# A hybrid attention, recurrence and gated feed-forward block: w_mod's sums moved out of the first and last pair, the out product finished row tile by row tile, and the rows of up begun among the transposes

## The reference

```python
mod = silu(c) @ w_mod + b_mod                      # 2048 x 12288
sh1, sc1, g1, sh2, sc2, g2 = split(mod, 6)         # 2048 numbers each
h = rms_norm(x, pre_mix_norm) * (1 + sc1) + sh1
q_a, k_a, v_a, f_b, q_b, i_b, g_b, gate_a, gate_b = split(h @ w_in)
y_a = sliding_window_sink_attention(q_a, k_a, v_a) @ w_branch_a
y_b = hgrn2_output(hgrn2_chunkwise(q_b, f_b, i_b), g_b) @ w_branch_b
merged = sigmoid(gate_a) * y_a + sigmoid(gate_b) * y_b
x = x + g1 * rms_norm(merged @ w_out, post_mix_norm)
h = rms_norm(x, pre_ffn_norm) * (1 + sc2) + sh2
a, b = split(h @ w_up)                             # 5504 columns each
y = (gelu(conv3(a) + conv_b) * b) @ w_down
x = x + g2 * rms_norm(y, post_ffn_norm)
```

## Time and profile before

| | |
|---|---|
| median of 3 runs | 2906.93 us (2905.8 to 2908.78) |
| the profiled execution | 2907.6 us, span 2905.9 us |
| mean granted TensorE clock | 0.986 |
| TensorE busy | 2820.5 us (97%), 13213 matmuls |
| VectorE busy | 1478.0 us (51%) |
| ScalarE busy | 1012.6 us (35%) |
| GpSimd busy | 36.6 us (1%) |
| HBM | 130 GB/s over the span |

### The profile page before, as it was taken

How to read it: one execution, slowest core, us unless ns; L and a number is a source line. 1 busy time by engine, 2 the same in 40 slices (tenths; PEclk the granted TensorE clock), 3 DMA queues, 4 the chain that set the end, 5 groups by cost and what they waited for, 6 DMA issues and landing times.

```text
span 2905.9 us, 36602 instructions
## 1 busy us (share of the span) xinstructions
PE 2820.5 (97%) x13213; PEld 2355.6 (81%) x13213; DVE 1478.0 (51%) x2011; ACT 1012.6 (35%) x1315; POOL 36.6 (1%) x74
## 2 busy tenths in 40 slices
PE   5999999999899999999989999999999999999997
PEld 5788888888788888878778888888888887888886
DVE  7857777778866666652253333333333333333334
ACT  4344444444422222232253333333333332323323
POOL 0030000000000000000000000000000000000000
PEclk8999999999899999999989999999999999999999
DMA  9842222223577777763233333333333334223222
GB/s 363 290 124 80 77 77 79 80 80 88 152 211 218 215 216 216 221 228 101 87 135 97 94 100 95 94 101 94 94 100 94 96 99 150 96 94 101 94 94 100
DMA packets 451695, 379.56 MB, mean 131 GB/s; under 512 B 20252, under 2 KB 376867, under 8 KB 448817
## 3 DMA queue, kind: packets, MB, share of 16 engines
q1 hardware_dynamic: 438624, 357.61, 40.2%
q0 software_dynamic: 3104, 16.93, 1.6%
q10 hardware_dynamic: 9904, 4.26, 0.6%
HBM read 368.25 MB, written 10.50 MB: 130 GB/s over the span
## 4 chain that ended last, share of the span: by engine, by line
PE 94%; DVE 3%; issue 1%; ACT 1%; DMA 1%; SPq 0%; DVEq 0%; ACTq 0%
PE acc_bank L480 24%; PE acc_bank L482 24%; PE acc_bank L481 24%; PE two_banks L480 2%; PE two_banks L481 2%; PE two_banks L482 2%; PE bank_pb L480 1%; PE bank_pb L481 1%; PE bank_tb L480 1%; PE bank_pb L482 1%; PE bank_ta L480 1%; PE bank_tb L481 1%; PE bank_tb L482 1%; PE bank_ta L481 1%; PE bank_ta L482 1%
## 5 line engine op out<-in xcount | busy, mean ns | idle before, releaser
L456 DVE TENSOR_TENSOR w_lo<-raw,w_hi 128x1024 fp32r<-128x1024 f32 x466 | 570.0, 1223 | 1235.7 <-ACT w_hi L450 1235.6
L450 ACT CAST w_hi<-raw 128x1024 fp32r<-128x1024 f32 x466 | 490.0, 1052 | 1491.7 <-PE acc_bank L482 972.7
L480 PE MATMUL acc_bank<-h_hi,w_hi 128*128 128x512 f32 x2500 | 983.5, 393 | 6.4 <-DVE h_lo L1287 6.4
L482 PE MATMUL acc_bank<-h_hi,w_lo 128*128 128x512 f32 x2500 | 975.0, 390 | 0.0
L481 PE MATMUL acc_bank<-h_lo,w_hi 128*128 128x512 f32 x2500 | 974.4, 390 | 0.0
L480 PEld LDWEIGHTS acc_bank<-h_hi,w_hi 128*128 128x128 f32 x2500 | 470.7, 188 | 101.3 <-issue 6.5
L482 PEld LDWEIGHTS acc_bank<-h_hi,w_lo 128*128 128x128 f32 x2500 | 470.1, 188 | 98.8
L481 PEld LDWEIGHTS acc_bank<-h_lo,w_hi 128*128 128x128 f32 x2500 | 470.7, 188 | 95.5
L1273 DVE SCALAR_TENSOR_TENSOR acc<-raw,csil,acc 128x512 f32<-128x512 f32 x240 | 180.0, 750 | 14.2 <-DMA raw<-in_w_mod_dram 7.6
L480 PE MATMUL acc_bank<-w_hi,a_hi 128*128 128x512 f32 x258 | 100.5, 389 | 2.8 <-DVE w_lo L456 2.8
L480 PE MATMUL acc_bank<-o_hi,w_hi 128*128 128x512 f32 x256 | 102.2, 399 | 0.8 <-DVE w_lo L456 0.8
(11 more groups left out here) (374 smaller groups left out, 3176.7 us busy)
## 6 DMA issues: line engine op xcount, KB each, us to landing
raw<-in_w_ffn_up_dram SPq DMA_DIRECT2D x172, 512.0 KB, 3.7
raw<-in_w_in_dram SPq DMA_DIRECT2D x148, 512.0 KB, 4.0
raw<-in_w_mod_dram SPq DMA_DIRECT2D x128, 512.0 KB, 4.5
raw<-in_w_ffn_down_dram SPq DMA_DIRECT2D x86, 512.0 KB, 3.6
mods_low<-in_w_mod_dram SPq DMA_DIRECT2D x32, 512.0 KB, 9.6
raw<-in_w_out_dram SPq DMA_DIRECT2D x32, 512.0 KB, 3.8
mods_hi<-in_w_mod_dram SPq DMA_DIRECT2D x16, 512.0 KB, 9.8
mods_lo<-in_w_mod_dram SPq DMA_DIRECT2D x16, 512.0 KB, 9.8
```

The lines of the kernel that those rows point to most:

```text
L450: act.copy(w_pair(g)[0][:], raw[n % RAW][:]).then_inc(hi_ready, 1)
L456: dve.tensor_tensor(w_l[:], raw[n % RAW][:], w_h[:].bitcast(F32), ALU.subtract).then_inc(lo_ready, 1)
L480: pe.matmul(o, stat[0], mov[0], start=start, stop=False)
L482: return pe.matmul(o, stat[1], mov[0], start=False, stop=stop)
```

## The change

* **w_mod.** Pair 0 and pair 7 carry no w_mod; pair 7 leaves the loop. Pairs 1 to 6 carry the 96 pieces of g1, sh2 and sc2.
* **g2 in up.** The 32 pieces of g2 are loaded by POOL, one in each of up's passes 1 to 32, into `small[:, 2:4]` (`g2_in`), issued when VectorE's products of the pass before are done. VectorE clears `gain2` and adds the products of four groups into its four quarters (`g2_piece`, between `w_lo` of pieces 0 and 1). After up, TensorE sums all 16 columns; at the start of down, VectorE forms `gcol`, TensorE transposes it at the fifth bank, ScalarE copies it to `acc` ahead of its split of the second piece, and POOL stores it and reads it back.
* **Out's last group.** Its first three pieces run as before. The last five have weight pairs of their own (three lie where h was) and are gone through once for each row tile, so that tile 0's sums are complete after 30 of 120 matmuls. Squares, products, root, inverse, x2, its squares and its root run tile by tile.
* **Transposed rows.** VectorE multiplies x2 itself by the inverse root (in place, once its store has landed; tile 3 in quarters into `x2_last`), and TensorE makes plain transposes into six banks. `diag` is gone.
* **Up's first pass.** Pieces 0 and 1 of up have weight pairs of their own and are split while tile 3 is normed. The rows of a and b are multiplied k by k, with the transposes of block kb + 6 behind those of kb.

```diff
 N2 = N1 + HEADS * HEAD_PIECES
-N3 = N2 + KT // 2 * (PAIR_PIECES + PAIR_MODS)
+MODS_PAIRS = 6
+NM = N2 + PAIR_PIECES - (PAIR_PIECES + PAIR_MODS)
+N3 = N2 + KT // 2 * PAIR_PIECES + MODS_PAIRS * PAIR_MODS
+MODS_LAST = MODS_HEAD + MODS_PAIRS * PAIR_MODS
+SUMS_LAST = MODS_LAST // 8
...
+            if OUT_KEPT < g < P4 - 1:
+                return RH[1]["out_hi"][:, g - OUT_KEPT - 1], RH[1]["out_lo"][:, g - OUT_KEPT - 1]
+            if g == P4 - 1:
+                return w_hi[OUT_KEPT % SPL - 1], w_lo[OUT_KEPT % SPL - 1]
+            if P4 <= g < P4 + 2:
+                return RO[5]["up_hi"][:, g - P4], RO[5]["up_lo"][:, g - P4]
             return w_hi[g % SPL], w_lo[g % SPL]
...
+        def pair_free(g, looped=0):
+
+            if not looped:
+                if OUT_KEPT < g < P4 - 1:
+                    return P3
+                if g == P4 - 1:
+                    return OUT_KEPT
+                if P4 <= g < P4 + 4:
+                    return P4
...
+            pair(0, True, False)
+            with pe.Fori(1, KT // 2 - 1) as it:
                 pair(it, False)
...
+            pair(KT // 2 - 1, False, False)
+
+            def turn_gains(n):
+
+                pe.wait_ge(gcol_ready, n + 1)
+                pe.transpose(SC1[0:KT, 0:P], gcol[:, n, :], ident[:]).then_inc(gcol_turned, 1)
...
+            out_group(P3, even_free(0), 0)
+            out_group(P3 + 8, odd_free, 1)
+            out_group(P3 + 16, even_free(1), 0)
+            out_group(P3 + 24, last_free, 1, 3)
+
+            for t4 in range(TT):
+                for g in range(OUT_KEPT, P4):
+                    if t4 == 0:
+                        pe.wait_ge(lo_ready, g + 1)
+                    wh, wl = weights(g, 2)
+                    for k in range(2):
+                        kb = 2 * (g - P3 - 24) + k
+                        mm = three(OUT_BANKS[1][t4], (m_hi[:, kb, t4 * P:(t4 + 1) * P], m_lo[:, kb, t4 * P:(t4 + 1) * P]),
+                                   (wh[:, k, :], wl[:, k, :]), False, kb == KT - 1)
+                    if t4 == TT - 1:
+                        mm.then_inc(multiplied, 1)
+                if t4 < TT - 1:
+                    mm.then_inc(y1_done, 1)
+
...
+            def turn(kb, i):
+                if i == TT - 1 and kb % 4 == 0:
+                    pe.wait_ge(x2n_ready, TT + kb // 4)
+                src = x2_last if i == TT - 1 else y1[:, i, :]
+                return pe.transpose(TURN6[kb % 6][:, i * P:(i + 1) * P], src[:, kb * P:(kb + 1) * P], ident[:])
+
...
+            pe.wait_ge(y1_out, 16)
+            for i in range(TT - 1):
+                pe.wait_ge(x2n_ready, i + 1)
+                for kb in range(5):
+                    turn(kb, i)
             pe.wait_ge(y1_out, 17)
...
+            for i in range(TT - 1):
+                turn(5, i)
+            for kb in range(6):
+                turn(kb, TT - 1).then_inc(h2_turned, 1)
+
+            def up_rows(b, kb):
+                g = P4 + 2 * (kb // 8) + b
+                wh, wl = weights(g, 8)
+                mm = three(A[b][:], (wh[:, kb % 8, :], wl[:, kb % 8, :]), (h_hi[:, kb, :], h_lo[:, kb, :]), kb == 0, kb == KT - 1)
+                if kb % 8 == 7:
+                    mm.then_inc(multiplied, 1)
+
+            pe.wait_ge(lo_ready, P4 + 2)
+            for kb in range(8):
+                pe.wait_ge(h2_ready, kb + 1)
+                up_rows(0, kb)
+                up_rows(1, kb)
+                turn_all(kb + 6)
+            pe.wait_ge(lo_ready, P4 + 3)
+            for kb in range(8, KT):
+                pe.wait_ge(h2_ready, kb + 1)
+                up_rows(0, kb)
+                if kb + 6 < KT:
+                    turn_all(kb + 6)
+            pe.wait_ge(lo_ready, P4 + 4)
+            for kb in range(8, KT):
+                up_rows(1, kb)
+
+
...
+            pe.wait_ge(mod_ops, 2 * (MODS_LAST + 32))
+            for j in range(KT):
+                t = pe.matmul(SC0[:, j:j + 1], gain2[:, j * P:(j + 1) * P], ones[:, 0:1], start=True, stop=True)
+            t.then_inc(mod_summed, 1)
...
             for i in range(TT):
+                if i < TT - 1:
+                    act.wait_ge(y1_done, i + 1)
+                else:
+                    act.wait_ge(multiplied, P4)
+                if i:
+                    act.wait_ge(x2_sq, i)
+                square_out(3, i)
+                act.wait_ge(y_sum, i + 1)
+                A_(rms[:, i:i + 1], ssq[:, i:i + 1], ACT.Sqrt, scale=1.0 / D, bias=eps_c).then_inc(root_ready, 1)
+                if i == TT - 1:
+                    split_hi(act, P4, N4)
+                    split_hi(act, P4 + 1, N4 + 1)
                 act.wait_ge(x2_ready, i + 1)
-                A_(x2_junk[:], y1[:, i, :], ACT.Square, accum_out=ssq2[:, i:i + 1]).then_inc(x2_sq, 1)
+                act.wait_ge(y1_sq, 13 + i)
+                A_(small[:].rearrange("p a b -> p (a b)"), y1[:, i, :], ACT.Square, accum_out=ssq2[:, i:i + 1]).then_inc(x2_sq, 1)
                 act.wait_ge(x2_sq, i + 1)
                 A_(rms2[:, i:i + 1], ssq2[:, i:i + 1], ACT.Sqrt, scale=1.0 / D, bias=eps_c).then_inc(x2_root, 1)
-            split_hi(act, P4, N4)
-            split_hi(act, P4 + 1, N4 + 1)
...
@@ -1199,7 +1309,11 @@
                     if s == 0:
                         act.wait_ge(act_ready, FB - 1 if u < 2 else FB)
                     down(base + u)
+                    if u == 0 and s == 0:
+                        act.wait_ge(gcol_turned, 2)
+                        act.copy(acc[0:KT, 0:P], SC1[0:KT, 0:P]).then_inc(grow_ready, 1)
                     if u == 0 and s == 1:
+                        act.wait_ge(grow_stored, 32)
...
             for i in range(TT):
+                product(3, i)
+                dve.tensor_reduce(ssq[:, i:i + 1], ssg.rearrange("p (g t) -> p t g", t=4)[:, i:i + 1, :], AX.X, ALU.add).then_inc(y_sum, 1)
+                dve.wait_ge(root_ready, i + 2)
+                link(dve.reciprocal(rms[:, i:i + 1], rms[:, i:i + 1]))
+                dve.wait_ge(y1_out, 14 + i)
                 STT(y1[:, i, :], y1[:, i, :], rms[:, i:i + 1], x_again[:, i, :], ALU.mult, ALU.add).then_inc(x2_ready, 1)
-
-            for i in range(TT):
-                dve.wait_ge(x2_root, i + 1)
-                dve.reciprocal(rms2[:, i:i + 1], rms2[:, i:i + 1]).then_inc(x2_rms, 1)
-                dve.wait_ge(x2_rms, i + 1)
-                TS(diag[:, i, :], ident[:], rms2[:, i:i + 1], None, ALU.mult).then_inc(diag_ready, 1)
+                if i:
+                    dve.wait_ge(x2_root, i)
+                    dve.reciprocal(rms2[:, i - 1:i], rms2[:, i - 1:i]).then_inc(x2_rms, 1)
+                    dve.wait_ge(x2_rms, i)
+                    dve.wait_ge(x2_stored[i - 1], 16)
+                    TS(y1[:, i - 1, :], y1[:, i - 1, :], rms2[:, i - 1:i], None, ALU.mult).then_inc(x2n_ready, 1)
             split_lo(dve, P4, N4)
-            split_lo(dve, P4 + 1, N4 + 1)
+            dve.wait_ge(x2_root, TT)
+            dve.reciprocal(rms2[:, TT - 1:TT], rms2[:, TT - 1:TT]).then_inc(x2_rms, 1)
+            dve.wait_ge(x2_rms, TT)
+            for c in range(4):
+                TS(x2_last[:, 512 * c:512 * c + 512], y1[:, TT - 1, 512 * c:512 * c + 512], rms2[:, TT - 1:TT], None, ALU.mult
+                   ).then_inc(x2n_ready, 1)
+                if c == 0:
+                    split_lo(dve, P4 + 1, N4 + 1)
...
+            def g2_piece(q, it):
+
+                sums = gain2[:, 512 * q:512 * q + 512]
+                dve.wait_ge(g2_landed, it * 16)
+                for half in range(2):
+                    dve.wait_ge(mod_ops, 2 * (MODS_LAST - 1) + half + it * 2)
+                    STT(sums, g2_in[:, half, :], csil[:, ds(it * 2 + (half - 2 - 16 * q), 1)], sums, ALU.mult, ALU.add
+                        ).then_inc(mod_ops, 1)
+
+            dve.wait_ge(x2_stored[TT - 1], 16)
+            link(dve.memset(gain2[:], 0.0))
+            for q in range(4):
+                with dve.Fori(1 + 8 * q, 9 + 8 * q) as it:
+                    up(it, q)
+            with dve.Fori(33, FB) as it:
+                up(it)
...
+                    if u == 0 and s == 0:
+                        dve.wait_ge(mod_summed, SUMS_LAST + 1)
+                        link(TTe(modc[:, MOD_G2:MOD_G2 + KT], SC0[:, 0:KT], bmod_c[:, MOD_G2:MOD_G2 + KT], ALU.add))
+                        TTe(gcol[:, 1, :], modc[:, MOD_G2:MOD_G2 + KT], post_ffn_c, ALU.mult).then_inc(gcol_ready, 1)
...
+            pool.wait_ge(h2_ready, KT)
+            for q in range(4):
+                with pool.Fori(1 + 8 * q, 9 + 8 * q) as it:
+                    pool.wait_ge(mod_ops, 2 * MODS_LAST - 2 + it * 2)
+                    k0 = it * 2 - (2 + 16 * q)
+                    pool.dma_start(g2_in, w_mod_t[:, ds(k0, 2), (MOD_G2 + 4 * q) * P:(MOD_G2 + 4 * q + 4) * P]).then_inc(g2_landed, 16)
+            pool.wait_ge(grow_ready, 2)
+            pool.dma_start(g_scr[KT:2 * KT], acc[0:KT, 0:P]).then_inc(grow_stored, 16)
+            pool.wait_ge(grow_stored, 32)
```

(64 more changed lines are left out.)

252 lines of the change are left out of this document (127 added, 125 removed).

## The result

The changed kernel takes 2879.02 us (median of 4 runs, 2878.29 to 2880.74), the kernel before, on the same chip, 2907.46 (4 runs). The ratio is 0.9903, 95% interval 0.9886 to 0.9920: 28.4 us less. The profiled execution took 2878.8 us, its span 2877.2, against 2907.6 and 2905.9 before.

The account below looks back on a forecast made before the run. TensorE was taken as the bound (94% of the chain), so only its holes and lowered clock counted. The terms -16.3 - 1.8 - 11.1 + 1.3 = -27.9 from 2906.9 gave 2879.0 us, range 2870 to 2891.

Parts of the forecast that it names:

- The seam: From up to down: column sums fill TensorE's 2.76 us wait, then the transposed gain is late; 1.3 us more, 0.5 to 4.2.
- pair 0: First pair: without w_mod's 32 VectorE products and two sums, 106.0 us becomes 89.7; 16.3 us less, bounds 9.5 to 21.4.
- the way from out to up: Out's end to up's first block's end: 42.4 us against 53.5, so 11.1 less, bounds 7.9 to 14.0.
- the last pair: Last pair loses w_mod's two column sums, 1.8 us less; its VectorE products are worth nothing.
- the two long waits: Pair 0 before the change: TensorE waited 4.0 us for VectorE's S and 3.1 before w_mod's column sums.
- both half-clock stretches: Pair 0 before the change: granted clock at 0.50, 1.2 GHz, after each of two long waits; expected at 2.4 GHz afterwards.
- small waits: Pair 0 after the change: TensorE would wait 4.3 us in total, in seven small waits, leaving the clock high.
- The rival that the pair was held by its own chains: Pair 0: ScalarE's casts and o_lo take over, only 6 us gained there; 2889 us, 1 in 10.
- two rivals: Out to up: clock low through interleaved rows, 2891.5, 1 in 10; late x2 stores (10.1 us), 2882, 5 in 100.
- the rule of the Trainium skill: Out to up: two-port VectorE tensor_scalar and GpSimd exclude each other; stores start up to 1.2 us later, sum unchanged.
- Up's loop: 32 passes get a 512 KB POOL transfer and two VectorE products (1.5 us), hidden by VectorE's slack; priced at nothing.
- as a rival: Between up and down: the clock falls, 2.9 us allowed; 2882 us, 17 in 100.

Follow-up runs that it names:

- transposes-first run: Changed kernel with all sixteen blocks of transposes made before up's first row, not between its rows: 2879.79 us.
- the split: Changed kernel with 4 of g2's 16 column sums ahead of up's pass 34, 12 after up, ScalarE's gain copy one piece later: 2875.77 us.
- early clearing shifted: Changed kernel with 4 sums ahead of pass 34, two made twice, 12 after up, gain copy later, gain2 cleared before up's first convolution: 2878.53 us.
- the first experiment: Changed kernel with w_mod and its two sums back in pair 0, and pair 6 without them: 2892.14 us.
- all sums early: Changed kernel with all 16 column sums of g2 in up's loop ahead of pass 34, none between up and down: 2882.86 us.
- early clearing: Changed kernel with 4 sums ahead of pass 34, 12 after up, gain copy later, gain2 cleared ahead of up's first convolution: 2876.68 us.
- transposes first with the split: Changed kernel with 4 sums ahead of pass 34, 12 after up, gain copy later, all transposes before up's first row: 2876.25 us.
- split shifted: Changed kernel with 4 sums ahead of pass 34, two of them made twice, 12 after up, gain copy later: 2878.21 us.

## Why the prediction was right, and where its terms were off

The figure, 2879.0, met 2879.02, and that it met it so closely is luck: terms of opposite sign helped, and two of them aren't the change's. The seam cost 3.25 more than put down and pair 0 gained 0.7 less; the way from out to up gained 2.1 more, the last pair 0.5, out 1.3, and the start came 0.9 earlier.

- **Start**, -0.9, and **out**, -1.3, against nothing. Neither was meant to change, and both differ as much between profiles of kernels that are the same there. Pair 0 began anywhere from 689.5 to 692.0 us in the twelve profiles with the changed kernel's start. For out, the windows that begin 3.6 us ahead of its first matmul tell the same, here the changed kernel and the transposes-first run, against the earlier trace rows' window from 1270:

```profile
1251.00:1291.00 40.00, 36.77 (x156) 30.16 (x156) 20.40 (x28) 15.82 (x24) 3.23 (x6) 0.96 0.61 223
1250.40:1290.40 40.00, 36.77 (x150) 29.97 (x150) 19.49 (x27) 15.32 (x24) 3.24 (x6) 0.91 0.63 223
```

  In the kernel before, out's first 13 matmuls ran at half clock, in the changed kernel its first 7; six by 0.2 us are 1.2 of the 1.3. But out took 176.9 to 177.0 at a clock of 0.91 in three other profiles (transposes first with and without the split, early clearing shifted), 175.6 to 175.8 at 0.96 in eight, and 174.55 at 1.00 in one. So this gain can't be put down to the change: it comes and goes in kernels that share this stretch. I had read it as untouched, and nothing here speaks against that.
- **Pair 0**, -15.6 against -16.3. The step held: 24 us less on VectorE, the two long waits and both half-clock stretches go. 4.3 us of small waits were walked out (six, though the text says seven), and six of 4.0 are there. The kernel before had 105.75 and not 106.0. Shown by taking the products back (2892.1) and making them narrow (2879.6). The rival that the pair was held by its own chains is out.
- **Last pair**, -2.3 against -1.8. The sums were priced by their recorded 1.84; pair for pair they cost 2.2, as the first experiment shows.
- **Out to up**, -13.2 against -11.1: right in mechanism, mis-sized in four terms. Up's first row came after 11.5 us, not 12.1. A block of transposes costs 0.47 (1.83 less six matmuls of 0.2266), not 0.56, over ten blocks 0.9 less. The low clock cost 1.9 and not 2.9 (29.0 from first row to second block, less 21.8, 4.7 and a wait of 0.62): it was on during the early transposes already, and only 3.7 us of rows (1441.73 to 1445.4) ran under it. Against that, w_lo of the second block was 0.62 late, since clearing gain2 took 1.76 us and not about 1. The kernel before had 53.75 and not 53.5. The clock was back with the first matmul of the second pair of rows, and the x2 stores didn't come late, which disposes of two rivals. On the rule of the Trainium skill (SBUF — State Buffer, Who interferes with whom) that I had weighed: the trace agrees with it, since an issue of GpSimd that met VectorE's tensor_scalar ended with it, 0.7 us late (1.22 against 0.54), where up to 1.2 was allowed for; as worked out, it changed no term. That the kernel before has no such pair was a misreading, though a small one: the issue of its last x2 store (1464.78, 0.53 us) met two of the products that made `diag`, and the second took 0.35 us in place of 0.28.
- **Up's loop**, +0.1: the 64 products are hidden as worked out.
- **The seam**, +4.55 against +1.3: the term that failed. I had put the clock's fall there at 17 in 100, as a rival. The parts: sums of 3.49 at full clock (the transposes-first run) in place of 2.9 of silence, +0.6; the transposed gain between the matmuls 0.2 and the wait for a_lo 0.5, together the 1.3 of the prediction; the rest, 4.55 - 1.3 = 3.3, is the fall, for which I had allowed 2.9 as a bound. What I had leaned on was one silent wait of 2.76 us in one profile that left the clock alone. The runs showed that this proves little: the same silence brought a fall in another kernel.

What decides whether the clock falls here stays open. Theory A, length: the stretch of 16 sums in the seam had a fall in all six profiles that have it (the changed kernel twice and four of the experiments). It cost 3.3 us in five of them, seams of 13.0, and 1.6 less in the one where it came late, 11.4. Of the seams of 2.8 to 2.9 us four had a fall (all sums early, early clearing, the same shifted, transposes first with the split) and three had none (before, split, split shifted). A fall cost them about 1.6 us: 12 sums took 8.6 without and 10.1 to 10.2 with it. So length raises the odds, but does not settle them. Theory that the moment decides: two seams 0.07 us apart went opposite ways, though in kernels that differ in the early clearing. Theory B, that sums bring it down and silence doesn't, fell with the 2.76 us wait. Only profiled executions show where the clock falls. For the others there is its mean: in the split shifted the runs of 2875.7, 2876.5, 2880.0 and 2881.6 us had 0.992, 0.991, 0.990 and 0.989, so the slower ones had more of the low clock. Their 5.8 us can't all be the seam's 1.6; out's start alone varies by 2.5 us with the clock, and pair 0's clock fell in one of ten profiles. Chance from execution to execution, at several places, is what fits best, without a cause shown.

Splitting the sums is probably still worth having. By the traces it costs 0.95 us in up's loop and takes the seam from 13.0 to 8.6 or 10.2, so it saves 1.9 to 3.4. Its medians are below the changed kernel's 2880.45 on the same chip, by 4.7 without and 3.8 with the early clearing; the slowest run of the split alone (2878.92) is under that kernel's fastest there (2879.37), though the intervals of the ratios (0.9881 to 0.9912 and 0.9895 to 0.9925) overlap. Over the five kernels with the split, 20 runs have a mean of 2877.3; eight runs of the changed kernel 2879.8. The split alone, at 2875.8, is the fastest median measured here, faster than both kernels.

## What to carry to other kernels

Work that is nearly free in every pass of a loop needn't be so in its first, where the engine that carries it may still have the work of the stage before, as VectorE had the last head's here: walk that engine's queue in the first pass by itself. Where one long product ends a stage and the next stage needs row sums, let the last pieces run tile by tile, so that each tile's chain lies under the next tile's matmuls: here that was 18 us, and interleaving the transposes 0.4. Filling a wait of TensorE with tiny matmuls costs little by the sum of durations (0.6 us here), but the clock is a term of its own at each such hole, here nothing, 1.6 or 3.3 us; give it a chance, not a value, when one profile shows it left alone. A term that comes and goes in stages that the change doesn't touch (here 2.2 us of the 28.7) is no gain of the change.
